# Moving the softmax normalisation of a memory cross-attention into the split of its probabilities, and the low parts from GpSimd to VectorE

## The reference

```python
def memory_attention(q_mem, mem_n, w_mem_kv):
    ...
    s = jnp.einsum('bthd,bmhd->bhtm', q.astype(jnp.float32), k_m.astype(jnp.float32)) * (MEM_DH ** -0.5)
    p = jax.nn.softmax(s, axis=-1)
    o = jnp.einsum('bhtm,bmhd->bthd', p, v_m.astype(jnp.float32))
    return o.reshape(B, T, D_MEM)
```

## Time and profile before

| | us |
|---|---|
| median of 3 runs (1571.22 to 1571.52) | 1571.4 |
| the profiled execution | 1571.57 |
| its span, first to last instruction | 1570.1 |
| PE busy | 1442.4 (92% of the span) |
| PEld busy | 1042.9 (66%) |
| DVE busy | 746.9 (48%) |
| ACT busy | 577.3 (37%) |
| POOL busy | 334.9 (21%) |

### The profile page before, as it was taken

How to read it: one execution, slowest core, us unless ns; L and a number is a source line. 1 busy time by engine, 2 the same in 40 slices (tenths; PEclk the granted TensorE clock), 3 DMA queues, 4 the chain that set the end, 5 groups by cost and what they waited for, 6 DMA issues and landing times.

```text
span 1570.1 us, 28228 instructions
## 1 busy us (share of the span) xinstructions
PE 1442.4 (92%) x11714; PEld 1042.9 (66%) x11714; DVE 746.9 (48%) x1221; ACT 577.3 (37%) x973; POOL 334.9 (21%) x298
## 2 busy tenths in 40 slices
PE   3259699999999999999999999999999999999985
PEld 2238576766768676776867576676867676676752
DVE  2775626455361726445262635436172645526162
ACT  1344424344342424334242434434242433424231
POOL 1321303031220303122221303122030313122110
PEclk9679799999999999999999999999999999999998
DMA  8130100101020010102010010102001010201001
GB/s 339 56 134 2 41 1 28 54 13 67 0 80 0 27 53 27 53 0 80 0 63 17 27 53 18 62 0 80 0 27 53 27 53 0 80 0 54 1 28 67
DMA packets 15432, 69.32 MB, mean 44 GB/s; under 512 B 2352, under 2 KB 2480, under 8 KB 12848
## 3 DMA queue, kind: packets, MB, share of 16 engines
q1 hardware_dynamic: 15408, 68.98, 11.9%
HBM read 52.20 MB, written 16.78 MB: 44 GB/s over the span
## 4 chain that ended last, share of the span: by engine, by line
PE 82%; DVE 8%; ACT 3%; issue 3%; POOL 2%; DMA 1%; SPq 1%; ACTq 0%; POOLq 0%; DVEq 0%
PE bank L330 69%; PE bank L467 2%; PE bank L475 2%; PE bank L481 2%; PE bank L489 2%; PE bank L532 1%; DVE whl L836 1%; DVE arena L979 1%; DVE nm L988 1%; DVE arena L997 1%; POOL arena L1156 1%; ACT arena L715 1%; PE bank L383 1%; DVE arena L962 1%; DVE mx L985 1%
## 5 line engine op out<-in xcount | busy, mean ns | idle before, releaser
L330 PE MATMUL bank<-arena,whl 128*128 128x256 f16 x6144 | 683.8, 274 | 3.0 <-DVE whl L836 3.0
L330 PEld LDWEIGHTS bank<-arena,whl 128*128 128x128 f16 x6144 | 601.6, 98 | 84.5 <-issue 7.0
L330 PE MATMUL bank<-arena 128*128 128x512 f16 x1536 | 343.5, 381 | 12.3 <-DVE arena L856 12.3
L330 PEld LDWEIGHTS bank<-arena 128*128 128x128 f16 x1536 | 148.2, 98 | 184.8 <-issue 18.6
L947 DVE SCALAR_TENSOR_TENSOR arena<-arena 64x256 f32<-64x256 f32 x60 | 25.2, 420 | 411.9 <-POOL arena L1173 410.5
L330 PE MATMUL bank<-whl,arena 128*128 128x512 f16 x768 | 168.4, 379 | 0.0
L676 ACT ACTIVATE arena<-bank,sca 128x512 f32<-128x512 f32 x64 | 43.9, 687 | 262.8 <-PE bank L330 261.7
L330 PEld LDWEIGHTS bank<-whl,arena 128*128 128x128 f16 x768 | 75.1, 98 | 87.3
L1156 POOL TENSOR_TENSOR arena<-arena 128x512 f16<-128x512 f32 x64 | 89.5, 1410 | 142.3 <-ACT arena L724 142.3
L1166 POOL TENSOR_TENSOR arena<-arena 128x542 f32<-128x542 f32 x16 | 17.3, 1079 | 463.9 <-issue 438.8
L867 DVE SCALAR_TENSOR_TENSOR arena<-bank,sca,arena 128x512 f32<-128x512 f32 x64 | 47.8, 749 | 108.0 <-PE bank L330 91.4
(11 more groups left out here) (154 smaller groups left out, 1516.0 us busy)
## 6 DMA issues: line engine op xcount, KB each, us to landing
arena<-in_xt SPq DMA_DIRECT2D x16, 1024.0 KB, 5.4
arena<-in_x SPq DMA_DIRECT2D x32, 512.0 KB, 3.4
out<-arena SPq DMA_DIRECT2D x32, 512.0 KB, 2.6
arena<-in_w_in SPq DMA_DIRECT2D x8, 768.0 KB, 16.1
arena<-in_w_out SPq DMA_DIRECT2D x1, 4096.0 KB, 12.2
arena<-in_w_in SPq DMA_DIRECT2D x8, 392.0 KB, 16.2
arena<-in_w_mem SPq DMA_DIRECT2D x1, 2048.0 KB, 10.9
arena<-in_memt SPq DMA_DIRECT2D x1, 1024.0 KB, 6.5
```

Source lines behind the costliest of these rows:

```text
L330: mm = nc.tensor.matmul(ap, lhs, rhs, start=k == 0 and n == 0, stop=(k, n) == last)
```

## The change

ACT's high part no longer waits for a normalised `pr`: it waits for the reciprocal and takes it as the scale of the rounding, one instruction for each head because each head has its own reciprocal. DVE no longer multiplies `pr`. It makes the low part itself, with `scalar_tensor_tensor` (probability by reciprocal, less the high part), again one instruction for each head, in a new function `p_low(n)` that waits for `p_hi`. POOL has no part in it any more.

```diff
@@ ACT
                 def p_hi_of(n):
-                    act.wait_ge(pn_ok, 4 * i + n + 1)
+                    act.wait_ge(rs_ok, 4 * i + n + 1)
                     if n >= 2:
                         act.wait_ge(pe_pt, 4 * i + n - 1)
-                    nc.scalar.activation(phl[n % 2][:, 0, :, :], pr[n % 2], ACT.Copy).then_inc(p_hi, 1)
+                    for h in range(2):
+                        a = nc.scalar.activation(phl[n % 2][:, 0, h, :], pr[n % 2][:, h, :], ACT.Copy,
+                                                 scale=rsum[:, 2 * n + h:2 * n + h + 1])
+                    a.then_inc(p_hi, 1)
@@ DVE
                     dve.wait_ge(p_exp, 4 * i + n + 1)
                     nc.vector.reciprocal(rsum[:, 2 * n:2 * n + 2], psum_p[:, 2 * n:2 * n + 2]).then_inc(rs_ok, 1)
-                    dve.wait_ge(rs_ok, 4 * i + n + 1)
-                    r = rsum[:, 2 * n:2 * n + 2].unsqueeze(2).broadcast_to([P, 2, NMEM])
-                    nc.vector.tensor_tensor(pr[n % 2], pr[n % 2], r, ALU.mult).then_inc(pn_ok, 1)
+
+                def p_low(n):
+
+                    dve.wait_ge(p_hi, 4 * i + n + 1)
+                    for h in range(2):
+                        a = nc.vector.scalar_tensor_tensor(phl[n % 2][:, 1, h, :], pr[n % 2][:, h, :],
+                                                           rsum[:, 2 * n + h:2 * n + h + 1], phl[n % 2][:, 0, h, :],
+                                                           ALU.mult, ALU.subtract)
+                    a.then_inc(p_lo, 1)
@@ DVE, the order in the block
                 p_norm(0)
                 p_norm(1)
+                p_low(0)
+                p_low(1)
                 rows(0)
                 state(0)
                 state(1)
...
                 pt_copy(0, 6)
                 p_norm(2)
                 p_norm(3)
+                p_low(2)
                 rows(1)
                 state(2)
                 pt_copy(1, 7)
+                p_low(3)
                 state(3)
@@ POOL
-            def p_lo_of(i, n):
-                pool.wait_ge(p_hi, 4 * i + n + 1)
-                nc.gpsimd.tensor_tensor(phl[n % 2][:, 1, :, :], pr[n % 2], phl[n % 2][:, 0, :, :],
-                                        ALU.subtract).then_inc(p_lo, 1)
...
-                for n in range(4):
-                    p_lo_of(i, n)
```

## The result

The changed kernel is slower: a median of 1591.03 us over 4 runs (1590.13 to 1591.67) against 1571.46 (1571.22 to 1572.31) for the kernel before on the same chip, a ratio of 1.0123 with a 95% interval of 1.0106 to 1.0141. The forecast was 1591.0.

A forecast was written before the change was run, and what follows sets the result against it. PE, busy 92%, bounds the kernel; the change adds a wait at its third transposes: 14 x 1.26 = 17.6, plus 0.5, plus 1.3, is 19.4 us on 1571.57, giving 1591.0. Range 1583 to 1599 (8 in 10), full bounds 1573 and 1601.

The forecast's parts named there:

- Step 1: ACT's high parts in a loop block: start 0.09 us after the accumulator read, a pair taking 0.92 us.
- Step 2: DVE's low part 0 is done sooner than POOL's was, so PE's first transposes start 0.27 us earlier.
- Step 3: On DVE, rows(0), two states and both maxima stand behind low part 1; rows(0) starts 1.62 us later.
- Steps 4 and 5: Late maxima delay piece 2's high and low parts; PE's third transposes start 1.26 us late, waiting about 1.5.
- The covers: Later in the block, low part 3 keeps 1.9 us before PE needs it, the residual rows over 5 us.
- The totals: Engine busy time: ACT's total grows by 4 x 0.29 us, DVE's hardly at all; both have idle time.
- The sum: Whole kernel: 14 x 1.26 us, plus 0.5 in the last block and 1.3 in the first, is 19.4 us.
- No change: Rival: pairs near their lower bounds, delay at the third transposes under 0.2 us, 1571.6 us; chance 0.05.
- faster: Rival: low parts in time for the third transposes, only 14 x 0.27 us gain stays, 1567.8 us; chance 0.04.
- The first rival's mechanism: POOL off SBUF stops slowing DVE between low part 1 and pt_copy(0), making the kernel faster; chance 0.04.
- The clock: Rival: PE's clock halves after a 1.5 us wait, doubling quarter(2), 15 x 5.3 us, 1671 us; chance 0.02.

The follow-up runs named there:

- e7: Changed kernel, DVE order alone: mem_max(2), mem_max(3) and pt_copy(0) directly behind p_low(1), rows(0) and the states later; 1569.23 us, ratio 0.9982.
- e8: Changed kernel, ACT and DVE reordered: high part 0 before exponential 1, low part 0 before p_norm(1), maxima before rows(0); 1565.11 us, ratio 0.9956.
- e2: Changed kernel, DVE order alone: rows(0) ahead of low part 0, both states behind the maxima of pieces 2 and 3 and pt_copy(0); 1570.93 us, ratio 0.9994.
- e9: Changed kernel plus one unused DVE maximum over 128x512 values between p_low(1) and rows(0); 1612.32 us, ratio 1.0261.
- e10: Changed kernel plus two unused DVE maxima over 128x1024 values ahead of p_low(3), in all blocks but the first; 1592.57 us, ratio 1.0134.
- e6: Kernel before the change, DVE's two states moved behind both maxima and pt_copy(0), POOL still making the low parts; 1574.2 us, ratio 1.0017.

## Why the prediction was right

- **Step 1, the high parts.** Right: the pair takes 0.90 us (0.92 predicted), an instruction 0.500, and the first starts 0.09 behind the accumulator read. The row that it was priced from, L597, differs in the type that it writes too (float32, the high part float16), and not in the function alone. The Trainium skill (ScalarE: Activation LUTs, What ACT_TABLE_LOAD costs) gives 0.893 us for the pair by the estimate in the prediction, and the trace's 0.90 agrees.
- **Step 2, the gain.** Right in place and size: T1 from 3.31 to 3.03 against 0.27 predicted. That it could be had was shown by e7 and e8.
- **Step 3, the queue.** `rows(0)` moved by 1.58 us (3.60 instead of 2.02 behind the first reciprocal), 1.62 predicted. It was the right cause: the same instructions in another order take the loss away (e2, e7), and a dose at this place arrives in full (e9).
- **Steps 4 and 5.** T3 moved by 1.23, predicted 1.26; the wait, predicted 1.5, is 1.51 by start times: the transposes before it start at 801.03, eight take 0.45 to the next start, and the next start at 802.99. The profile notes 1.35 because it counts from the modelled end of those eight, 801.64.
- **The covers.** Low part 3 had 1.9 us, as predicted (it ends at 806.97, PE needs it at 809.05 less 0.15). e10 shows that there is room. The instruction that waits for the residual rows' load starts 3.7 us later in its block than before (23.14 against 19.48 behind the first reciprocal), where the prediction had 3.2, and something unforeseen came of it (last section), inside the 5 us: the loop block grew by 1.23, just as T3 did.
- **The totals.** ACT was to grow by 18.6 us (16 x 4 x 0.29) and grew by 13.1. DVE was to grow hardly at all and grew by 27.1. Of its groups, the low parts in place of the multiplications have 5.0 more (55.0 against 50.0), and one product that collided with POOL has 24.6 more (35.5 against 10.9, last section); groups overlap at their edges, so they add up to more than the total. This error of the prediction cost nothing, because DVE has idle time there.
- **The sum.** It fits to 0.1 us by luck: its errors cancel. The span grew by 19.6 us. The 14 loop blocks have 17.2 of it (14 x 1.23), 17.6 predicted. Block 0 has 0.65 instead of 1.3; the transposes were late by 1.25 and 1.4 there, and 0.64 of that was given back by PE's clock. The eight matmuls of L481 behind the fourth transposes take 1.79 us before and 1.15 after (the rows below). The kernel before is there earlier, while the granted clock is still 0.50 (173.40 to 174.60 us); after, the clock has risen by then (0.82 from 174.80 to 175.40, 0.50 until 174.80). The last block and what follows it have 1.65 instead of 0.5: 0.42 at the transposes, 0.4 because DVE reaches the maximum of the mixed rows later, and about 0.8 in the final output projection, whose first matmuls ran at half clock for longer (the granted clock of the first 11.2 us from its start is 0.83 before and 0.74 after). The last is a matter of when the clock rises, and it varies between kernels: the stage from the last block's first reciprocal to the end is 71.1 us before, 72.7 after, and 71.8 in e2, whose last block has its transposes where before had them.

```profile
173.39 1.79 PE L481 MATMUL bank<-arena 128*128 128x128 f32 x8
...
174.82 1.15 PE L481 MATMUL bank<-arena 128*128 128x128 f32 x8
```

- **The rivals.** No change, and faster, did not happen. The first rival's mechanism, POOL slowing DVE, had nothing to give in the stretch that decides: the states and the maximum of piece 2 take 1.31 and 0.68 us after, 1.30 and 0.68 before. e6 shows the mechanism at work in another order. The clock got too low a chance, since 0.6 us more of waiting was enough to bring it, and too high a price: e9 lost 1.69 us in every second block, not 5.3 in each.

## What to carry to other kernels

Work moved to another engine takes effect through what stands behind it in that engine's queue: read what the next consumer waits for, several instructions later, not the engine's share. In an order written by hand, put first what starts the next round trip (here the maxima, on which ACT and then PE wait) and let the work that is needed late (states, residual rows) fill the gaps; the same instructions then ran in 1569 or 1565 instead of 1591 us. A move that loses in the place where it was put may win with the order changed around it, so try the order before undoing the move.

## What the runs showed that was not expected

The granted clock of PE held at 2.4 GHz with a wait of 1.35 us at T3 in every block (1.23 us of another wait stand some 16 us ahead of it), and fell to 1.2 GHz behind every second one when that wait was 1.94 us (e9). A wait on PE can so cost twice: itself and 1.69 us behind it. The stretch of the loop in the kernel after, for comparison (busy times, granted clock third from the right):

```profile
200.00:1560.00 1360.00, 1308.25 (x10770) 943.24 (x10769) 645.12 (x1124) 513.00 (x935) 208.03 (x189) 1.00 0.09 33
```

The clock was a rival with 0.02; the margin to it was at most 0.6 us of waiting.

The Trainium skill (TensorE: Matmul & The Clock Gate, HAM oscillation) describes such falls behind longer waits, on transfers. The trace agrees in kind, but here the fall came behind a wait of 1.94 us, and for VectorE.

DVE and POOL collided in a place that had been free. In the kernel after, the late residual rows (L870) push DVE's product of the pooling branch (L1075, two inputs in SBUF) under POOL's low parts of the input (L1133, the second of the two again by itself in the last row):

```profile
815.52 0.75 DVE L870 SCALAR_TENSOR_TENSOR arena<-bank,sca,arena 128x512 f32<-128x512 f32 x1 [2.94 <-DMA arena<-in_x]
816.19 2.44 DVE L1075 TENSOR_TENSOR arena<-arena 128x512 f32<-128x512 f32 x1
818.55 0.74 DVE L1077 SCALAR_TENSOR_TENSOR arena<-bank,sca,arena 128x512 f32<-128x512 f32 x1
```

```profile
815.95 4.66 POOL L1133 TENSOR_TENSOR arena<-arena 128x1024 f16<-128x1024 f32 x2 [22.86 <-ACT arena L611]
...
818.04 2.58 POOL L1133 TENSOR_TENSOR arena<-arena 128x1024 f16<-128x1024 f32 x1
```

L1075 takes 2.44 us, where the same product took 0.68 before. It ends 0.55 us behind POOL's first instruction, which takes 2.13 as before and ends at 818.08; POOL's second takes 2.58 instead of 2.12. So it looks as if DVE waited for the first and POOL's second for DVE. L1077, with one input in PSUM, stands beside POOL's second instruction and keeps its 0.74.

The Trainium skill (SBUF — State Buffer, Who interferes with whom) says that a DVE instruction with two SBUF inputs contends with a GpSimd instruction that reads SBUF, and the trace agrees.

This happens in the 14 loop blocks and makes most of the 27.1 us by which DVE's busy time grew. The time of the kernel doesn't show it: `rows(3)`, DVE's next instruction for PE, still waits 0.75 us for PE at 820.04.
